# Fetching the modulation slabs four by four between weight slabs in the head of a two-block transformer kernel

## The chip, the cores and the metric

The kernel runs on one core of a Trainium2 chip. The metric is device time in microseconds (us) of one execution. The engines are TensorE (PE in the rows; PEld is its weight load), VectorE (DVE), ScalarE (ACT), GpSimd (POOL) and SyncE (SP). The rows mark with a q what an engine's queue only issues: SPq and ACTq are transfers that SyncE and ScalarE start.

## What is computed

Two layers of a first block and two of a second, over 256 tokens of width 1024, in fp32. The part that the change touches is the very start of the first layer of the first block:

```
silu_c, silu_cc = silu(c), silu(c_ctx)
shift, scale, gate = split(silu_c @ w_mod[l] + b_mod[l], 3)       # for x
shift_c, scale_c, gate_c = split(silu_cc @ w_mod[l] + b_mod[l], 3)  # for ctx
hc = rms_norm(ctx) * g_pre[l] * (1 + scale_c) + shift_c
zc = hc @ w_in[l]           # 1024 x (11*512 + 3072), then heads, attention, merge
...
ctx = ctx + gate_c * rms_norm(c_out, g_post[l])
```

`w_mod[l]` is 1024 x 3072: a third of it gives the shift, a third the scale, a third the gate. Shift and scale are needed before any column of `hc @ w_in` can be finished; the gate only when the layer closes.

## The kernel before, in words

All large matrices are fetched from HBM in slabs of 512 KB, 256 rows (two k-tiles of 128) by 512 columns. A weight slab lands in one of four places of `raw` (`SLOTS`). ScalarE copies it to `whi` (rounded to fp32r, `split`, L550), GpSimd writes the remainder `wlo = raw - whi` (L525) and raises `lo_ready`. TensorE multiplies each 128x128 tile of the activations (`hhi`, `hlo`) with `whi` and `wlo` in three products (L1890 to L1892), 12 matmuls of 512 columns to a slab, and raises `weights_used`. SyncE may fetch weight slab n only when GpSimd has finished slab n-4 (`slab`, L413), and it is one queue in order: a transfer that has to wait holds back all that are written behind it.

The first pass starts with weight slabs 0 to 11 (`first_chunks`), three chunks of columns (RK, RQ, DKc) times four slabs. Each chunk is split in two halves of k: slabs 0 to 5 are k-tiles 0 to 3 of the three chunks, (c, s) = (0,0) (0,1) (1,0) (1,1) (2,0) (2,1), and slabs 6 to 11 are k-tiles 4 to 7, (0,2) (0,3) (1,2) (1,3) (2,2) (2,3). From slab 12 on the chunks are whole: 12 to 15 are DQ, 16 to 19 RV, and so on.

The modulation slabs (`w_mod`) are counted here as M0, M1, ... M0 to M7 give shift and scale of the first half of k, M8 to M15 those of the second half; they land in eight places of `modz`, and TensorE multiplies them with the conditioning vectors (`mod_slab`, L2066). The sum is copied by ScalarE (`mod_copy`, L723), turned by TensorE (`mod_turn`, L2075), and VectorE makes `modT` of it (L1252, L1253). ScalarE and VectorE then write the high and the low part of the activations of a quarter of k (`stream_high` L613, `stream_low` L1185 and L1188), after TensorE has turned that quarter (`turn_tokens`, L1956). M16 and on are the gate columns and later chunks: they land in three places of `modw`, and VectorE accumulates them (L1219, L1221), one slab being four operations. M19 and later ones wait on SyncE until VectorE has used the slab three before (`modw_used`). `MOD_FIRST` says how many modulation slabs SyncE fetches behind each of weight slabs 0 to 11, `MOD_BESIDE` the same for later ones: in this pass M19 stands behind weight slab 12, M20 behind 13, M21 behind 15, M22 behind 17.

VectorE does stream_low of all four quarters and then M16 to M19. TensorE turns the gate rows behind weight slab 12 and waits there until M19 is used (`turn_rows`, L2122, L2125).

ScalarE's program around this: split 4, split 5, split 6, mod_copy, split 7, three transfers (const, dist, wsT), the streams of quarters 2 and 3 with splits 8 and 9 behind them, then split 10, evacuation of RK (two tiles, L754), split 11, split 12, evacuation of RQ, split 13, split 14, evacuation of DKc, split 15. Behind that come the eight exponentials of the decay tables and the reach values (`decays`, L774 and L775, `reach`, L789), with no split between them, and then splits 16, 17 and 18.

Of the kernel before, what the change touches and what calls it, by code (L numbers as in the profile page):

```python
# [143 lines left out]
def build(nc, g, out):  # L144
# [14 lines left out]
    with ExitStack() as ctx:  # L159
        def sem(name):  # L160
            return ctx.enter_context(nc.semaphore(name))
# [171 lines left out]
        mod_turned, modT_ready = sem("mod_turned"), sem("modT_ready")  # L333
# [55 lines left out]
                  (4, 0): (8, 9), (4, 1): (10, 11, 12), (4, 2): (6, 7)}  # L389
        MOD_ORDER = (0, 2, 1, 3)  # L390
        HALVES = [[(c, s) for c in range(3) for s in part] for part in ((0, 1), (2, 3))]
        MOD_FIRST = {(1, 1): 3, (2, 0): 1, (2, 1): 4, (0, 3): 1, (1, 3): 1, (2, 3): 1}
        MOD_BESIDE = {0: (12, 13, 15, 17, 22, 23, 25, 26, 30, 31, 32, 33, 35), 1: (3, 4, 5, 14, 17, 18, 22, 23),
                      3: (3, 4, 5, 18, 19, 22, 23, 24)}
        LATE = [MV, RG, DG, MU, MG]
# [12 lines left out]
        def _(sp):  # L408
            w = Tally(sp)

            def slab(mat, row, col, slot, n=CH):

                sp.wait_ge(lo_ready, w(lo_ready))  # L413
                src = mat[bass.ds(row, SLAB_K * P), bass.ds(col, n)].rearrange("(k p) n -> p k n", p=P)
                sp.dma_start(raw[:, slot, :, 0:n], src).then_inc(raw_full[slot], 16)
# [11 lines left out]
            def mod_slab():  # L427

                i = mods["n"]
                mods["n"] += 1  # L430
                l, r = divmod(i, 6 * SLOTS)
                c, q = divmod(r, SLOTS)
                if i < 4 * SLOTS:
                    c = MOD_ORDER[c]
                src = flat["w_mod"][l * D + q * SLAB_K * P:l * D + (q + 1) * SLAB_K * P, c * CH:(c + 1) * CH]
                src = src.rearrange("(k p) n -> p k n", p=P)
                if i < 4 * SLOTS:
                    if i >= MODZ:
                        sp.wait_ge(mod_used, w(mod_used))
                    sp.dma_start(modz[:, i % MODZ], src).then_inc(modz_full[i % MODZ], 16)  # L440
                else:
                    if i >= 4 * SLOTS + MODW:
                        sp.wait_ge(modw_used, w(modw_used))
                    sp.dma_start(modw[:, i % MODW], src).then_inc(modw_full[i % MODW], 16)
# [5 lines left out]
            def first_chunks():  # L450

                for n, (c, s) in enumerate(HALVES[0] + HALVES[1]):
                    slab(flat["w_in"], s * SLAB_K * P, (RK, RQ, DKc)[c], n % SLOTS)
                    for _ in range(MOD_FIRST.get((c, s), 0)):
                        mod_slab()
# [84 lines left out]
        def _(act):  # L540
            w = Tally(act)
# [6 lines left out]
            def split(slot, n=CH):  # L548
                act.wait_ge(raw_full[slot], w(raw_full[slot], 16))
                act.activation(whi[:, slot, :, 0:n], raw[:, slot, :, 0:n], ACT.Copy).then_inc(hi_ready, 1)  # L550
# [53 lines left out]
            def turned_high(scale, shift, banks=HB, quarters=range(4), high=h_pairs[0]):  # L604

                for q in quarters:
                    act.wait_ge(h_turned, w(h_turned))
                    for k in range(2 * q, 2 * q + 2):
                        part = banks[q][:, (k % 2) * S:(k % 2 + 1) * S]
                        if shift is None:  # L610
                            ins = act.activation(high[q][:, k % 2], part, ACT.Copy, scale=scale(k))
                        else:
                            ins = act.activation(high[q][:, k % 2], part, ACT.Identity, scale=scale(k), bias=shift(k))  # L613
                    ins.then_inc(h_high, 1)

            def stream_high(n, quarters):

                a = 0 if PASSES[n][0] else 1
                turned_high(lambda k: modT[:, 1, k, a:a + 1], lambda k: modT[:, 0, k, a:a + 1], HB_FIRST if n == 0 else HB_EDGE,
                            quarters, (h_ctx_pairs if n == 2 else h_pairs)[0])  # L620
# [99 lines left out]
            def mod_copy():  # L720

                act.wait_ge(mod_used, w(mod_used, 2 * SLOTS))
                act.activation(modrow[:], A[2][:, 0:MODN], ACT.Copy).then_inc(mod_copied, 1)  # L723

            def first_chunks():

                mod_copy()
                split(0)
                act.wait_ge(modT_ready, w(modT_ready))
                for q in range(2):  # L730
                    stream_high(0, (q,))
                    split(1 + q)
                split(3)
                for slot in range(2):
                    act.wait_ge(weights_used, w(weights_used))
                    split(slot)
                for slot in range(2, 4):
                    act.wait_ge(weights_used, w(weights_used))
                    split(slot)
                    if slot == 2:  # L740
                        mod_copy()
                act.dma_start(const[:, N_FIRST:], g["p_const"][:, N_FIRST:]).then_inc(consts_in, 16)
                tables(0)
                act.wait_ge(modT_ready, w(modT_ready))
                for q in range(2):
                    stream_high(0, (2 + q,))
                    act.wait_ge(weights_used, w(weights_used))
                    split(q)
                for c, col in enumerate((RK, RQ, DKc)):
                    act.wait_ge(weights_used, w(weights_used))  # L750
                    split((2 * c + 2) % SLOTS)
                    for t in range(TT):
                        act.wait_ge(projected, w(projected))
                        act.activation(z[:, t, col:col + W], (G[0:2], G[2:4], A[0:2])[c][t][:], ACT.Copy).then_inc(evacuated, 1)  # L754
                    split((2 * c + 3) % SLOTS)
# [1129 lines left out]
        def _(pe):  # L1885
            w = Tally(pe)
# [63 lines left out]
            def turn_tokens(src, banks, quarters):  # L1950

                for q in quarters:
                    for b in range(2):
                        k = 2 * q + b
                        for t in range(TT):
                            ins = pe.transpose(banks[q][:, b * S + t * P:b * S + (t + 1) * P], src[:, t, k * P:(k + 1) * P], ident)  # L1956
                    ins.then_inc(h_turned, 1)
# [120 lines left out]
            def first_chunks():  # L2078

                def part(n, c, s, fresh=False):  # L2080
                    pe.wait_ge(lo_ready, w(lo_ready))
                    if fresh:
                        pe.wait_ge(h_split, w(h_split))
                    banks = (G[0:2], G[2:4], A[0:2])[c]
                    for t in range(TT):
                        for kk in range(SLAB_K):
                            k = s * SLAB_K + kk
                            cols = slice(t * P, (t + 1) * P)
                            ins = product(banks[t][:], hhi[:, k, cols], hlo[:, k, cols], n % SLOTS, kk, CH, k == 0, k == KT - 1)
                        if s == SLOTS - 1:  # L2090
                            ins.then_inc(projected, 1)
                    if s < SLOTS - 1:
                        ins.then_inc(weights_used, 1)

                pe.wait_ge(silu_c, w(silu_c))
                for i in range(2 * SLOTS):
                    if i == 5:
                        pe.wait_ge(ident_in, w(ident_in, 16))
                        pe.wait_ge(norm_ready, w(norm_ready, TT))
                        turn_tokens(normed, HB_FIRST, (0, 1))  # L2100
                    mod_slab(A[2])
                pe.wait_ge(mod_copied, w(mod_copied))
                mod_turn(A[2], modrow)
                for r in range(28):
                    pe.transpose(A[3][:, r % 4 * P:(r % 4 + 1) * P], normed[:, 0, r % 8 * P:(r % 8 + 1) * P], ident)
                for n, (c, s) in enumerate(HALVES[0]):
                    part(n, c, s, c == 0)
                    for _ in range((0, 0, 5, 3, 0, 0)[n]):
                        mod_slab(A[2])
                    if n == 3:  # L2110
                        turn_tokens(normed, HB_FIRST, (2,))
                        pe.wait_ge(mod_copied, w(mod_copied))
                        mod_turn(A[2], modrow)
                    if n == 4:
                        pe.wait_ge(modT_ready, w(modT_ready, 2))
                        turn_tokens(normed, HB_FIRST, (3,))
                for n, (c, s) in enumerate(HALVES[1]):
                    part(n + len(HALVES[0]), c, s, c == 0)
# [545 lines left out]
```

## Time and profile before

| | |
|---|---|
| three timed runs | 1803.73, 1803.93 and 2532.1 us, median 1803.93 |
| the profiled execution | 1803.99 us, of which 1802.0 us is the span from the first to the last instruction |
| around the span | 1.99 us |
| mean granted TensorE clock | 0.999 of full speed |
| TensorE busy | 99% of the span |

The times are of the whole program; the change touches only what is queued in the first 60 us of it. All times of instructions below are from the start of the span of the profiled execution. "Idle before" in a row is the time that the engine stood still ahead of that instruction, and the arrow names who ended it.

### The profile page before, as it was taken

How to read it: one execution, taken by the hardware profiler on the slowest of the kernel's cores; microseconds unless marked ns; L12 is line 12 of the kernel's file. 1: busy time of each engine (PE TensorE's matmuls, PEld its weight loads, DVE VectorE, ACT ScalarE, POOL GpSimd, SP SyncE). 2: the span in 40 equal slices, each digit the busy share in tenths (PEclk: the TensorE clock that was granted, in tenths of full speed). 3: DMA queues.
4: the chain of work that ended last, by engine and by line, in shares of the span. 5: the costliest groups of instructions: out<-in, count | busy, mean ns of one | idle time of the engine just before them, and what ended most of it. 6: DMA issues, size and time to landing. Idle time of an engine off the chain costs nothing.

```text
span 1802.0 us, 25383 instructions
## 1 busy us (share of the span) xinstructions
PE 1782.7 (99%) x9224; PEld 1488.9 (83%) x9224; DVE 763.7 (42%) x1340; ACT 1047.3 (58%) x1560; POOL 1360.9 (76%) x573
## 2 busy tenths in 40 slices
PE   7999999999999999999999999999999999999998
PEld 4888888888888888888888878898888878888887
DVE  2782344843334546343337374321113665431112
ACT  4645675445677654466655666565555566746554
POOL 5867787866778877676879766778887865688886
PEclk9999999999999999999999999999999999999999
DMA  9875556754556667454647544556555654456663
GB/s 367 288 256 161 167 175 205 234 158 139 154 178 189 179 204 233 139 151 151 193 134 224 152 129 140 175 167 195 187 190 173 192 143 130 148 178 196 187 186 128
DMA packets 171409, 327.88 MB, mean 182 GB/s; under 512 B 10416, under 2 KB 15792, under 8 KB 171312
## 3 DMA queue, kind: packets, MB, share of 16 engines
q1 hardware_dynamic: 168272, 320.49, 57.6%
q10 hardware_dynamic: 3040, 6.06, 0.9%
q8 instruction: 66, 1.08, 0.2%
q14 instruction: 31, 0.25, 0.0%
HBM read 325.46 MB, written 1.05 MB: 181 GB/s over the span
## 4 chain that ended last, share of the span: by engine, by line
PE 67%; POOL 16%; issue 16%; ACT 0%; POOLq 0%; DVE 0%; DMA 0%; ACTq 0%; DVEq 0%
POOL wlo L525 16%; PE G L1890 15%; PE G L1892 15%; PE G L1891 15%; PE A L2596 2%; PE G L2596 2%; PE A L1890 2%; PE A L1892 2%; PE A L1891 2%; PE A L2597 1%; PE G L2597 1%; PE A L2342 1%; PE G L2364 1%; PE A L1944 1%; PE A L2227 1%
## 5 line engine op out<-in xcount | busy, mean ns | idle before, releaser
L525 POOL TENSOR_TENSOR wlo<-raw,whi 128x1024 fp32r<-128x1024 f32 (+1 forms) x568 | 1357.2, 2400 | 427.2 <-ACT whi L550 424.5
L550 ACT ACTIVATE whi<-raw 128x1024 fp32r<-128x1024 f32 (+1 forms) x568 | 593.1, 1048 | 571.6 <-PE G L1892 423.8
L1890 PE MATMUL G<-whi,hparts 128*128 128x512 f32 (+1 forms) x1472 | 582.3, 396 | 1.6 <-DVE hparts L1276 0.6
L1892 PE MATMUL G<-whi,hparts 128*128 128x512 f32 (+1 forms) x1472 | 568.2, 386 | 0.0
L1891 PE MATMUL G<-wlo,hparts 128*128 128x512 f32 (+1 forms) x1472 | 567.8, 386 | 0.0
L1890 PEld LDWEIGHTS G<-whi,hparts 128*128 128x128 f32 x1472 | 276.5, 188 | 60.3 <-issue 5.2
L1892 PEld LDWEIGHTS G<-whi,hparts 128*128 128x128 f32 x1472 | 276.4, 188 | 57.0
L1891 PEld LDWEIGHTS G<-wlo,hparts 128*128 128x128 f32 x1472 | 276.8, 188 | 50.9
L1890 PE MATMUL G<-whi,osplit 128*128 128x512 f32 x240 | 94.2, 393 | 0.0
L1892 PE MATMUL G<-whi,osplit 128*128 128x512 f32 x240 | 93.4, 389 | 0.0
L1891 PE MATMUL G<-wlo,osplit 128*128 128x512 f32 x240 | 93.4, 389 | 0.0
L1825 DVE TENSOR_TENSOR G<-G,frelu 128x512 f32<-128x512 f32 x12 | 8.4, 699 | 188.9 <-ACT frelu L1119 188.9
L1606 DVE TENSOR_REDUCE nmx<-A 128x1 f32<-128x512 f32 (+1 forms) x48 | 25.6, 595 | 112.3 <-PE A L2342 112.2
L2596 PE MATMUL A<-hparts,whi 128*128 128x512 f32 x192 | 70.0, 398 | 0.0
L2596 PE MATMUL G<-hparts,whi 128*128 128x512 f32 x192 | 69.9, 398 | 0.0
L1221 DVE SCALAR_TENSOR_TENSOR A<-modw,cond,A 128x512 f32<-128x512 f32 x84 | 60.0, 753 | 9.3 <-DMA modw<-in_w_mod 7.6
L586 ACT ACTIVATE z<-G 128x512 f32<-128x512 f32 x66 | 39.5, 599 | 33.3 <-PE G L1892 33.1
L2597 PE MATMUL A<-hparts,wlo 128*128 128x256 f32 x192 | 53.9, 281 | 0.0
L2597 PE MATMUL G<-hparts,wlo 128*128 128x256 f32 x192 | 53.9, 281 | 0.0
L1892 PEld LDWEIGHTS G<-whi,osplit 128*128 128x128 f32 x240 | 45.1, 188 | 9.4
L1890 PEld LDWEIGHTS G<-whi,osplit 128*128 128x128 f32 x240 | 45.1, 188 | 9.4 <-issue 0.3
L1891 PEld LDWEIGHTS G<-wlo,osplit 128*128 128x128 f32 x240 | 45.1, 188 | 9.1
(413 smaller groups left out, 2558.6 us busy)
## 6 DMA issues: line engine op xcount, KB each, us to landing
raw<-in_w_in SPq DMA_DIRECT2D x324, 512.0 KB, 3.8
raw<-in_w_up SPq DMA_DIRECT2D x64, 512.0 KB, 3.7
raw<-in_w_down SPq DMA_DIRECT2D x64, 512.0 KB, 3.5
raw<-in_w_out SPq DMA_DIRECT2D x40, 512.0 KB, 3.9
raw<-in_w_branch_out SPq DMA_DIRECT2D x36, 512.0 KB, 4.3
modw<-in_w_mod SPq DMA_DIRECT2D x32, 512.0 KB, 5.1
raw<-in_w_branch SPq DMA_DIRECT2D x24, 512.0 KB, 3.5
modz<-in_w_mod SPq DMA_DIRECT2D x16, 512.0 KB, 10.0
```

The costliest lines, as they stand in the source:

```text
L525: pool.tensor_tensor(wlo[:, s, :, 0:n], raw[:, s, :, 0:n], whi[:, s, :, 0:n].bitcast(F32), ALU.subtract)\
L550: act.activation(whi[:, slot, :, 0:n], raw[:, slot, :, 0:n], ACT.Copy).then_inc(hi_ready, 1)
L586: act.activation(dst[c][t], banks[t][:], func, scale=1.0 if scale is None else scale[t])\
L1221: ins = dve.scalar_tensor_tensor(kept if k == KT - 1 else bank[:], part, row, bank[:], ALU.mult, ALU.add)
L1606: ins = dve.reduce_max(nmx[:, i, b:b + 1], A[2 * i + b][:, 0:nk], AX.X, negate=True)
L1890: pe.matmul(bank, hi, whi[:, slot, kk, 0:n], start=first, stop=False)
L1891: pe.matmul(bank, hi, wlo[:, slot, kk, 0:n], start=False, stop=False)
L1892: return pe.matmul(bank, lo, whi[:, slot, kk, 0:n], start=False, stop=last)
L1944: ins = pe.transpose(A[n % 4][:, b * S + t * P:b * S + (t + 1) * P], srcs[2 * (n - bank) + b](t), ident)
L2227: ins = pe.transpose(bank[:, b * S + t * P:b * S + (t + 1) * P], z[:, t, c + h * P:c + (h + 1) * P], ident)
L2596: pe.matmul(bank, whi[:, s, kk, cols], hparts[:, :, k], start=k == 0, stop=False, skip_group_check=True)
L2597: ins = pe.matmul(bank[:, 0:S], wlo[:, s, kk, cols], hhi[:, k], start=False, stop=k == KT - 1, skip_group_check=True)
```

## The change

The modulation slabs M8 to M15 are fetched four behind weight slab 3 and four behind weight slab 4. Before it was three behind slab 3, one behind 4, four behind 5. M16, M17 and M18 are fetched behind slab 10 (one) and slab 11 (two). Before, one each stood behind slabs 7, 9 and 11. TensorE multiplies M8 to M11 behind weight slab 3 and M12 to M15 behind weight slab 4 (before: five behind slab 2, three behind slab 3). mod_turn moves from behind slab 3 to behind slab 4, and the turning of quarter 3 from behind slab 4 to behind slab 5. On ScalarE the second mod_copy moves ahead of split 6, the stream of quarter 2 ahead of split 7, and quarter 3 ahead of split 8. The number of instructions and of bytes stays.

```
-        MOD_FIRST = {(1, 1): 3, (2, 0): 1, (2, 1): 4, (0, 3): 1, (1, 3): 1, (2, 3): 1}
+        MOD_FIRST = {(1, 1): 4, (2, 0): 4, (2, 2): 1, (2, 3): 2}
...
                 for slot in range(2):
                     act.wait_ge(weights_used, w(weights_used))
                     split(slot)
+                mod_copy()
                 for slot in range(2, 4):
                     act.wait_ge(weights_used, w(weights_used))
                     split(slot)
                     if slot == 2:
-                        mod_copy()
+                        act.wait_ge(modT_ready, w(modT_ready))
+                        stream_high(0, (2,))
                 act.dma_start(const[:, N_FIRST:], g["p_const"][:, N_FIRST:]).then_inc(consts_in, 16)
                 tables(0)
-                act.wait_ge(modT_ready, w(modT_ready))
-                for q in range(2):
-                    stream_high(0, (2 + q,))
+                stream_high(0, (3,))
+                for slot in range(2):
                     act.wait_ge(weights_used, w(weights_used))
-                    split(q)
+                    split(slot)
...
                 for n, (c, s) in enumerate(HALVES[0]):
                     part(n, c, s, c == 0)
-                    for _ in range((0, 0, 5, 3, 0, 0)[n]):
+                    for _ in range((0, 0, 0, 4, 4, 0)[n]):
                         mod_slab(A[2])
                     if n == 3:
                         turn_tokens(normed, HB_FIRST, (2,))
+                    if n == 4:
                         pe.wait_ge(mod_copied, w(mod_copied))
                         mod_turn(A[2], modrow)
-                    if n == 4:
+                    if n == 5:
                         pe.wait_ge(modT_ready, w(modT_ready, 2))
                         turn_tokens(normed, HB_FIRST, (3,))
```

## Rows read from the trace of the kernel before

**Rows 1.** Page, part 1 (busy time) and part 5 (last column: idle before).

```profile
PE 1782.7 (99%) x9224; PEld 1488.9 (83%) x9224; DVE 763.7 (42%) x1340; ACT 1047.3 (58%) x1560; POOL 1360.9 (76%) x573
...
L1890 PE MATMUL G<-whi,hparts 128*128 128x512 f32 (+1 forms) x1472 | 582.3, 396 | 1.6 <-DVE hparts L1276 0.6
```

**Rows 2.** Timeline of TensorE, 30 to 76 us: start, duration, instruction, idle before.

```profile
30.97 1.93 PE L2066 MATMUL A<-modz,cond 128*32 128x256 f32 x32
33.63 0.64 PE L2066 MATMUL A<-modz,cond 128*32 128x256 f32 x8 [0.73 <-DMA modz<-in_w_mod]
...
40.47 0.62 PE L2075 MATMUL A<-const,modrow 128*128 128x16 f32 x4 [1.23 <-ACT modrow L723]
...
46.99 0.39 PE L1890 MATMUL G<-whi,hparts 128*128 128x512 f32 x1
...
66.04 1.03 PE L2125 MATMUL A<-const,modacc 128*128 128x128 f32 x8
...
75.82 0.47 PE L1890 MATMUL G<-whi,hparts 128*128 128x512 f32 x1 [0.57 <-POOL wlo L525]
```

**Rows 3.** Timeline of ScalarE, 29 to 75 us.

```profile
29.60 1.06 ACT L550 ACTIVATE whi<-raw 128x1024 fp32r<-128x1024 f32 x1 [5.20 <-DMA raw<-in_w_in]
...
39.09 1.06 ACT L550 ACTIVATE whi<-raw 128x1024 fp32r<-128x1024 f32 x1 [5.72 <-DMA raw<-in_w_in]
...
60.79 1.06 ACT L550 ACTIVATE whi<-raw 128x1024 fp32r<-128x1024 f32 x1 [1.17 <-PE A L1892]
...
63.51 0.60 ACT L754 ACTIVATE z<-A 128x512 f32<-128x512 f32 x1 [0.76 <-PE A L1892]
...
64.96 0.68 ACT L774 ACTIVATE A<-dist,lg 128x512 f32<-128x512 f32 x1
...
71.95 2.94 ACT L550 ACTIVATE whi<-raw 128x1024 fp32r<-128x1024 f32 x3
```

**Rows 4.** Stretches of 10 us: busy time by engine, clock, DMA share, GB/s.

```profile
30.00:40.00 10.00, 8.51 (x85) 4.89 (x83) 0.00 (x0) 2.63 (x3) 4.75 (x2) 1.00 1.05 387
40.00:50.00 10.00, 9.53 (x46) 7.95 (x47) 7.08 (x12) 5.42 (x9) 8.81 (x4) 1.00 1.05 397
```

**Rows 5.** Timeline of GpSimd, at 31 us.

```profile
30.74 2.37 POOL L525 TENSOR_TENSOR wlo<-raw,whi 128x1024 fp32r<-128x1024 f32 x1 [1.67 <-ACT whi L550]
```

**Rows 6.** Tile raw on SyncE's queue, around 54 and 62 us: issue and landing.

```profile
L415 SPq DMA_DIRECT2D raw<-in_w_in x1: 444/444/444, 54.0 to 54.0; - x1
...
DMA to landing us min/median/max: 6.0/6.0/6.0
...
L415 SPq DMA_DIRECT2D raw<-in_w_in x1: 367/367/367, 62.1 to 62.1; - x1
...
DMA to landing us min/median/max: 3.8/3.8/3.8
```

**Rows 7.** Transfers issued in the first 100 us: KB each, median us to landing.

```profile
dist<-in_k_dist ACTq DMA_DIRECT2D x1, 768.0 KB, 8.0
const<-in_p_const ACTq DMA_DIRECT2D x1, 456.0 KB, 6.4
...
wsT<-in_mlp_w_s ACTq DMA_DIRECT2D x1, 256.0 KB, 11.3
```

**Rows 8.** Timeline of SyncE's queue: the issue of M19 and of M20.

```profile
50.64 0.37 SPq L444 DMA_DIRECT2D modw<-in_w_mod  x1
...
53.54 0.37 SPq L444 DMA_DIRECT2D modw<-in_w_mod  x1
```

**Rows 9.** Timeline of VectorE: second half of modT, first decay operation.

```profile
41.33 1.30 DVE L1253 SCALAR_TENSOR_TENSOR modT<-modT,small 128x8 f32<-128x8 f32 x1
...
66.41 0.70 DVE L1448 TENSOR_TENSOR A<-A,e 128x512 f32<-128x512 f32 x1 [6.96 <-ACT e L775]
```

**Rows 10.** Two stretches at the end of the span, columns as in rows 4.

```profile
1796.00:1798.70 2.70, 0.00 (x0) 0.00 (x0) 1.40 (x3) 1.53 (x4) 0.00 (x0) 1.00 0.00 0
1798.70:1802.00 3.30, 0.00 (x0) 0.00 (x0) 0.24 (x1) 0.21 (x1) 0.00 (x0) 0.51 0.42 159
```

More of the change, by code:

```diff
@@ L391, in build @@
         HALVES = [[(c, s) for c in range(3) for s in part] for part in ((0, 1), (2, 3))]
-        MOD_FIRST = {(1, 1): 3, (2, 0): 1, (2, 1): 4, (0, 3): 1, (1, 3): 1, (2, 3): 1}
+        MOD_FIRST = {(1, 1): 4, (2, 0): 4, (2, 2): 1, (2, 3): 2}
         MOD_BESIDE = {0: (12, 13, 15, 17, 22, 23, 25, 26, 30, 31, 32, 33, 35), 1: (3, 4, 5, 14, 17, 18, 22, 23),
@@ L736, in first_chunks @@
                     split(slot)
+                mod_copy()
                 for slot in range(2, 4):
@@ L740, in first_chunks @@
                     if slot == 2:
-                        mod_copy()
+                        act.wait_ge(modT_ready, w(modT_ready))
+                        stream_high(0, (2,))
                 act.dma_start(const[:, N_FIRST:], g["p_const"][:, N_FIRST:]).then_inc(consts_in, 16)
                 tables(0)
-                act.wait_ge(modT_ready, w(modT_ready))
-                for q in range(2):
-                    stream_high(0, (2 + q,))
+                stream_high(0, (3,))
+                for slot in range(2):
                     act.wait_ge(weights_used, w(weights_used))
-                    split(q)
+                    split(slot)
                 for c, col in enumerate((RK, RQ, DKc)):
@@ L2107, in first_chunks @@
                     part(n, c, s, c == 0)
-                    for _ in range((0, 0, 5, 3, 0, 0)[n]):
+                    for _ in range((0, 0, 0, 4, 4, 0)[n]):
                         mod_slab(A[2])
@@ L2111, in first_chunks @@
                         turn_tokens(normed, HB_FIRST, (2,))
+                    if n == 4:
                         pe.wait_ge(mod_copied, w(mod_copied))
                         mod_turn(A[2], modrow)
-                    if n == 4:
+                    if n == 5:
                         pe.wait_ge(modT_ready, w(modT_ready, 2))
```

## The prediction

> **What bounds the kernel now.** I read the page's busy shares first, then the timelines of TensorE and of ScalarE over the first 80 us, then the DMA share in stretches of 10 us and the landing of single transfers. TensorE is busy for 1782.7 of 1802.0 us [rows 1]. So nothing in the head can win more than the idle time that TensorE has there, while a new wait costs its whole length. From the first weight slab to slab 16 TensorE stands still three times [rows 2]: 0.73 us for M12, 1.23 us for ScalarE's copy of the modulation row, and 0.57 us at 75.82 for GpSimd's slab 16. The third is of another kind. ScalarE has the decay exponentials and the reach values between split 15 and split 16: they start at 64.96 and split 16 comes at 71.95 [rows 3], 7.0 us later, and TensorE starts slab 16 at 75.82, 3.87 us after that. So the start of slab 16 hangs on the end of split 15, not on TensorE's own pace: **slab 16 starts 10.86 us after the decays start.** TensorE's commonest matmul has 1.6 us of idle time before it in the whole run, the largest part that one releaser ended being 0.6 us [rows 1]; there is nothing behind slab 16 in which a delay could vanish, so a shift of slab 16 goes to the end of the kernel whole.
>
> The second thing to see is DMA: its share is 1.05 and it moves 387 to 397 GB/s between 30 and 50 us [rows 4]. A slab of 512 KB takes 1.36 us at 387 GB/s. Landings in this stretch are thus a sum of bytes in order of issue, and any time in which the queue runs empty is lost to all that land behind.
>
> **TensorE's side.** Slabs 0 to 2 end at 30.97 as before; then came five modulation slabs with the wait of 0.73 and three more. Four modulation slabs cost 1.93 us [rows 2], a weight slab 2.72 us ((66.04 - 46.99) / 7, slabs 6 to 12 [rows 2]). With the change slab 3 runs from 30.97 to 33.7, M8 to M11 (landed by 29.6, see below) to 35.7, the turn of quarter 2 (0.7) to 36.4, slab 4 to 39.1, M12 to M15 to 41.1. ScalarE then is free and copies at once, so the wait is some 0.5 us (a copy of 0.4 and the handing over) in place of 1.23. Slab 5 runs from 42.1 to 44.9, the turn of quarter 3 to 45.5. Slab 6 then has to wait for the low part of quarter 2, whose chain is: mod_turn 42.1, modT 42.6, stream_high behind split 6 to 43.8, stream_low (two operations and a subtraction, 1.8 us) to 45.7. That takes 0.3 us back. Slab 6 starts at 45.8, before 46.99 [rows 2]. **TensorE is 1.2 us earlier** from there, and slab 12 would end at 64.8, slab 15 at 73.8. The moved instructions cost nothing more: their number is the same, they stand on the same engines.
>
> **DMA's side.** Slab 4 landed at 29.6 and slab 6 at 39.1 (ScalarE's splits start there, released by DMA [rows 3]); slab 5, with M11 between, two slabs behind slab 4 at 32.3. Now one more modulation slab is ahead of slab 4 and four more are ahead of slab 5: they land at 31.0 and 37.7; slab 6 stays at 39.1, slab 7 at 40.4, slab 8, without M16 ahead, at 41.7. But slab 9 may only be issued when GpSimd is done with slab 5. Split (1.06 [rows 3]) and remainder (2.37 [rows 5]) take 3.5 us: 41.2. The fastest landing in this stretch is 3.8 us after the issue [rows 6], so slab 9 lands at 45.0, and between 41.7 and some 43 to 45 the queue holds nothing else: slab 10 waits for slab 6 (split after mod_copy, 41.5 to 42.6, remainder to 45.1), and M16 now stands behind slab 10. ScalarE's three transfers, 456, 768 and 256 KB [rows 7], were issued from 40.46 and are now issued behind split 7, from 43.7, data from 46.0.
>
> Before, by 44.4 slab 9 and M16 had landed. Now at 46.0 slab 9 is there and M16 is not: **DMA is 1.6 us and one slab (1.4 us) behind, 3.0 us in all.** Slab 14 landed at 60.0 (issued 54.0, 6.0 us [rows 6]), with the stretch before it full. All that stands ahead of it is the same set as before, so it comes at 60.0 + 3.0 = 63.0 at the earliest. A second gate acts on top: M19 is ahead of slab 13 and M20 ahead of slab 14 in SyncE's queue, and they wait for VectorE. The issues of M19 and M20 are 2.9 us apart [rows 8], which is VectorE's pace per slab. M16 lands at about 52.6: const takes from 46.0 to 47.2, slab 10 shares the engines with dist to 50.1, M16 with what is left of dist and with wsT to 52.6. So it is used at 55.5, M17 at 58.4, M18 at 61.2. M20 is issued at 58.4, lands no earlier than 62.2, and slab 14 a slab later at 63.5. **I take 63.4 for slab 14 and 64.8 for slab 15**; the ends are 61.5 (the gap in the queue half as long, M16 1 us earlier) and 66.
>
> **What follows on ScalarE.** Before, split 14 at 60.79 waited for TensorE, not for its data [rows 3]. Now it waits for data: 63.5 to 64.5, then the two evacuations of DKc (0.6 each [rows 3]) to 65.5, split 15 (data there at 64.8) 65.5 to 66.5. The decays start at 66.45 in place of 64.96: **+1.5 us**. Slab 16 starts at 66.45 + 10.86 = 77.3 in place of 75.82. TensorE will be done with slab 15 at 73.8, so the idle time there grows from 0.57 to 3.5 us, and what was won before (1.2 us) is inside it: the net is +1.5 us. The gate rows are late as well, and here I count nothing: M19 lands at 59.4, VectorE uses it by 64.0, TensorE asks behind slab 12 at 64.8. If that cover is gone the wait falls inside the same 3.5 us. VectorE itself stood idle for 6.96 us until 66.41 in the run before [rows 9], so being busy to 64.0 doesn't delay the decays. Slabs 12 and 13 have 0.3 to 1 us to spare, by the same landings; if they are late, that too is inside the 3.5 us.
>
> Sum: 1803.99 + 1.5 = **1805.5 us**. The profiled execution stands 0.06 us above the median of the runs shown, so it is used as it is.
>
> **A rule against the row.** The second modT operation, on 8 elements to a partition, took 1.30 us [rows 9]. It ended at 42.63, with GpSimd in the middle of its work. The Trainium skill, "SBUF — State Buffer", on the shared port pair, says that VectorE and GpSimd hold a common port pair for a whole instruction and that the other blocks. The trace agrees with that. By that rule the new order is lucky: GpSimd is idle between slab 5 (41.2) and slab 6 (from 42.6) when modT is written at 42.5, and the operation should take about 0.2. If the block hits after all, the stream, split 7 and ScalarE's transfers come 1 us later, and the sum would be about +2.3 instead of +1.5.
>
> **The rivals.**
> (1) *The landings don't hold ScalarE.* If slab 14 is there by 59.6 and slab 15 by 63, split 14 follows TensorE again and everything is 1.2 us earlier: 1802.8 us. What speaks for it: slab 14 landed 0.8 us before its split in the run before, and my DMA chain is long. Against: the queue needs 3 us less than I count. The point from which it decides is slab 14's landing at 61.9: earlier wins, later loses. Chance 0.23.
> (2) *Nothing to be seen*: the two shifts cancel, decays start within 0.4 us of 64.96, 1803.6 to 1804.4. Chance 0.15.
> (3) *The clock falls in the wait.* At the end of the span TensorE has no instruction after 1796, the granted clock is 1.00 until 1798.7 and then 0.51, 1.2 GHz in place of 2.4 [rows 10]. My wait ahead of slab 16 is 3.5 us, longer than those 2.7. If the clock falls, slab 16 takes up to 5.4 in place of 2.7 us and slab 17 part of it: +1.5 to +3 us on top of the +1.5, 1807 to 1808.5. Against: no wait of this size stands between matmuls in the trace, and where it lies in time may matter. Chance 0.12. The Trainium skill, "TensorE: Matmul & The Clock Gate", says the same of idle stretches: TensorE falls to half its clock after one. It speaks against this change; rows 10 show it only at the end of work.
>
> **How the numbers follow.** The forecast, 1804.5 to 1807, has 0.50, the rivals 0.23, 0.15 and 0.12. Eight tenths lie between 1802.5 (rival 1 reached) and 1808.0 (rival 3 in most of its reach, or the block in the port). Likeliest case alone: 1804.5 to 1807. About 2% is what a measurement of this kernel can tell from no change; that would be 36 us, and no mechanism here reaches it: within 2% has 0.98, the rest is left for something unseen, slightly more to the slow side.
>
> **What would show it.** Right: the timeline of TensorE has no wait at 33 us, about 0.5 us before mod_turn at 41.5, slab 6 at 45.8; DMA share has a dip between 42 and 46 us; ScalarE's split 14 is released by DMA and not by TensorE; the decays start near 66.5; TensorE's wait for wlo ahead of slab 16 is 3 to 4 us, and no later stretch differs. Wrong: a split 14 still released by TensorE (rival 1), a granted clock below 1.00 after 74 us (rival 3), a new wait of TensorE for slab 9 or for the gate rows, or a shift that appears only after 80 us. A slab 14 later than 66 would break the range upward.

## The result, and the profile after

The changed kernel takes 1808.19 us (median of 12 runs, 1807.59 to 1809.8) against 1803.77 us, a ratio of 1.0026 with a 95% interval of 1.0018 to 1.0033: 4.4 us slower, clear of noise. The prediction took 2% for what a measurement of this kernel can tell; the interval is under 0.1% to either side. Of the kernel before, eleven of twelve runs lie between 1803.59 and 1804.20 us and one took 2532.1 us, which the median leaves out. The forecast had the sign and the place, but 1.5 us for the size; the range ended at 1808.0, just short of the measured median. The profiled execution took 1809.39 us with a span of 1807.4 us, 5.4 us more than before, so it lies at the upper end of the runs. I account for that execution first, and for the median with the experiments.

TensorE's waits in the changed kernel, 22 us to the end (engine, line, released by: us in total, times, longest):

```profile
PE G L1891 <- POOL wlo L525: 4.3, 1, 4.3
PE G L1891 <- DVE hparts L1189: 0.6, 2, 0.4
PE G L1891 <- DVE hparts L1277: 0.6, 1, 0.6
PE A L2076 <- ACT modrow L723: 0.5, 1, 0.5
```

The waits for M12 (0.73) and the long one for the modulation row (1.23) of [rows 2] are gone and a short one for the row is left (0.5), as worked out. What was 0.57 us ahead of weight slab 16 is now 4.3 us. The same place in TensorE's timeline, with the idle time before and then the length of the matmuls behind it:

```profile
73.68 0.39 PE L1893 MATMUL G<-whi,hparts 128*128 128x512 f32 x1
78.39 0.77 PE L1891 MATMUL G<-whi,hparts 128*128 128x512 f32 x1 [4.32 <-POOL wlo L525]
78.96 0.63 PE L1892 MATMUL G<-wlo,hparts 128*128 128x512 f32 x1
```

Slab 16 starts at 78.39 in place of 75.82: +2.6 us. And the matmuls behind the wait last 0.63 us in place of 0.39. Their starts are 0.43 us apart, against 0.23 before. In stretches of 2 us, the column behind the busy times is the granted clock:

```profile
74.00:76.00 2.00, 0.07 (x1) 0.00 (x0) 1.97 (x5) 2.00 (x6) 0.32 (x1) 1.00 0.11 42
76.00:78.00 2.00, 0.00 (x0) 0.00 (x0) 2.00 (x2) 2.00 (x4) 2.00 (x1) 0.85 0.00 0
78.00:80.00 2.00, 1.61 (x4) 1.35 (x5) 1.97 (x4) 1.50 (x3) 2.00 (x2) 0.50 0.30 39
80.00:82.00 2.00, 2.00 (x7) 1.52 (x6) 1.93 (x4) 0.00 (x0) 2.00 (x2) 0.50 0.72 235
82.00:84.00 2.00, 2.00 (x7) 1.51 (x6) 1.96 (x4) 0.11 (x1) 2.00 (x2) 0.50 0.79 249
84.00:86.00 2.00, 2.00 (x11) 1.70 (x10) 1.96 (x3) 1.43 (x2) 1.99 (x2) 0.94 0.87 218
```

TensorE stands still from 74.07, its clock falls from 2.4 to 1.2 GHz within the stretch 76 to 78 and comes back at the start of 84 to 86. So it works at half speed from 78.4 to about 84.2: 5.8 us in which 2.9 us of work at full speed are done. 2.6 + 2.9 = 5.5 us, the 5.4 us of the span. The Trainium skill, "TensorE: Matmul & The Clock Gate", section "What's actually happening", puts an idle stretch ahead of a fall to the half clock; here the trace agrees, between matmuls and not only at the end.

Why slab 16 is late can be read on ScalarE's timeline (compare [rows 3]):

```profile
60.93 1.06 ACT L550 ACTIVATE whi<-raw 128x1024 fp32r<-128x1024 f32 x1 [0.86 <-DMA raw<-in_w_in]
64.70 1.06 ACT L550 ACTIVATE whi<-raw 128x1024 fp32r<-128x1024 f32 x1 [2.71 <-DMA raw<-in_w_in]
...
66.62 1.06 ACT L550 ACTIVATE whi<-raw 128x1024 fp32r<-128x1024 f32 x1
...
67.56 0.70 ACT L775 ACTIVATE A<-dist,lg 128x512 f32<-128x512 f32 x1
...
74.57 2.93 ACT L550 ACTIVATE whi<-raw 128x1024 fp32r<-128x1024 f32 x3
```

Split 14, at 60.79 and released by TensorE before, is at 64.70 and released by DMA. The decays start at 67.56 in place of 64.96 (+2.6), split 16 comes 7.0 us later as before, and TensorE starts slab 16 10.83 us after the decays (10.86 in the prediction).

On SyncE's queue, M19 and M20 (compare [rows 8]) and then SyncE's waits before and after, from 22 to 75 us:

```profile
55.60 0.37 SPq L444 DMA_DIRECT2D modw<-in_w_mod  x1
56.02 0.47 SPq L415 DMA_DIRECT2D raw<-in_w_in  x1
58.50 0.37 SPq L444 DMA_DIRECT2D modw<-in_w_mod  x1
```

```profile
SPq L444 <- DVE A L1221: 4.7, 2, 2.7
```

```profile
SPq L444 <- DVE A L1222: 9.1, 3, 5.6
```

M20 is issued at 58.50 in place of 53.54, and SyncE waits 9.1 us for VectorE in place of 4.7. The queue ran empty as expected, but from 40 us on, earlier than the 42 to 46 us of the prediction (compare [rows 4]; the last two columns are DMA share and GB/s):

```profile
40.00:42.00 2.00, 1.50 (x22) 0.91 (x11) 0.17 (x1) 1.26 (x2) 0.86 (x1) 1.00 0.06 16
42.00:44.00 2.00, 2.00 (x10) 1.65 (x9) 0.80 (x4) 1.83 (x4) 1.85 (x1) 1.00 0.84 257
```

How much that costs shows at slab 12, the last weight slab ahead of M19 and M20 in the queue. Its issue and its time to landing, before and after:

```profile
L415 SPq DMA_DIRECT2D raw<-in_w_in x1: 368/368/368, 47.6 to 47.6; - x1
...
DMA to landing us min/median/max: 7.2/7.2/7.2
```

```profile
L415 SPq DMA_DIRECT2D raw<-in_w_in x1: 368/368/368, 49.6 to 49.6; - x1
...
DMA to landing us min/median/max: 8.4/8.4/8.4
```

It lands at 58.0 in place of 54.8, 3.2 us late. Slab 14 lands at 64.6 in place of 60.0, 4.6 us late (its row stands in the account of the prediction below). So 3.2 us were lost before M19 was issued, and 1.4 us behind it.

### The profile page after: what moved, and what is told of

It is laid out like the page before. It is cut to its first block, busy times and chain, and to the rows that moved or that the text cites. A ratio compares the mean times of both kernels' runs of the same rounds, so it can differ in the third digit from the quotient of the medians.

```text
span 1807.4 us, 25383 instructions
## 1 busy us (share of the span) xinstructions
PE 1785.5 (99%) x9224; PEld 1490.5 (82%) x9224; DVE 766.2 (42%) x1340; ACT 1046.2 (58%) x1560; POOL 1360.4 (75%) x573
## 4 chain that ended last, share of the span: by engine, by line
PE 66%; POOL 16%; issue 16%; ACT 0%; POOLq 0%; DVE 0%; DMA 0%; ACTq 0%; DVEq 0%
POOL wlo L525 16%; PE G L1891 15%; PE G L1893 15%; PE G L1892 15%; PE A L2598 2%; PE G L2598 2%; PE A L1891 2%; PE A L1893 2%; PE A L1892 2%; PE A L2599 1%; PE G L2599 1%; PE A L2344 1%; PE G L2366 1%; PE A L1945 1%; PE A L2229 1%
## 5 line engine op out<-in xcount | busy, mean ns | idle before, releaser
L2599 PE MATMUL A<-hparts,wlo 128*128 128x256 f32 x192 | 53.9, 281 | 0.0
L2599 PE MATMUL G<-hparts,wlo 128*128 128x256 f32 x192 | 53.9, 281 | 0.0
```

Of the source, the lines that this page charges most:

```text
L2599: ins = pe.matmul(bank[:, 0:S], wlo[:, s, kk, cols], hhi[:, k], start=False, stop=k == KT - 1, skip_group_check=True)
```

## The experiments

The times are medians of 10 or 11 runs, with the lowest and the highest in brackets; the kernel before, run beside them, stood at 1803.68 to 1803.86 us. The 95% interval of a median's ratio to it reaches 0.0009 or 0.0010 to either side, 1.6 to 1.8 us. The changed kernel, also with the filled wait, and the very last version are clear of it. A difference of 1.5 us or less is shown by no interval here; it is read from the medians and the traces.

**The clock: fill the wait.** The changed kernel with work for TensorE ahead of slab 16 (c = 2 is the chunk of slabs 16 to 19).

```
                         pe.wait_ge(evacuated, w(evacuated, TT))
+                        for r in range(36 if c == 2 else 0):
+                            pe.transpose(G[0][:, r % 4 * P:(r % 4 + 1) * P], ident, ident)
```

> The changed kernel with 36 transposes of the identity into the free bank G[0] ahead of weight slab 16 (one such transpose took 0.12 us at full clock, so 4.2 us, inside TensorE's wait of 4.3 us there). They compute nothing that is used. Theory (the wait lets the clock fall, and the slow stretch is paid on top of the late slab): the granted clock stays 1.00 after 77 us, slab 16 still starts near 78.4, the idle time ahead of it is under 1 us, and the time is that of before plus 2.6 us, 1806.4 us, with less spread between runs than 1807.6 to 1809.8. Rival (the slow stretch costs nothing, as GpSimd is behind anyway and would hold TensorE at its own pace): the time stays at 1808.2 us.

Measured: 1807.67 us (1806.81 to 1808.31). Its trace, TensorE's timeline and then stretches of 2 us:

```profile
75.47 4.09 PE L2286 MATMUL G<-const 128*128 128x128 f32 x36
79.89 0.50 PE L1891 MATMUL G<-whi,hparts 128*128 128x512 f32 x1 [0.33 <-POOL wlo L525]
```

```profile
76.00:78.00 2.00, 2.00 (x21) 2.00 (x20) 1.97 (x5) 2.00 (x4) 0.75 (x1) 1.00 0.01 2
78.00:80.00 2.00, 1.67 (x16) 1.43 (x15) 2.00 (x1) 2.00 (x5) 2.00 (x2) 1.00 0.00 0
80.00:82.00 2.00, 2.00 (x9) 1.66 (x10) 1.93 (x5) 1.07 (x3) 2.00 (x1) 1.00 0.33 81
```

The clock stays full, as expected, but the time is 1.3 us above the theory's. In this execution slab 16 starts at 79.89, 4.1 us late and not 2.6. The transposes end at 79.56 and TensorE still waits 0.33 us for GpSimd, so they are not what holds it. The program ahead of them is that of the changed kernel, so the lateness itself changes from one execution to the next. This profiled execution took 1808.1 us, 4.4 us above the median of before, and 4.1 of it is slab 16. To separate the two parts I ran the changed kernel and the filled one once more, side by side.

> The changed kernel once more, nothing edited, beside its twin with the filled wait. Theory (the extra time has two parts, a slab 16 that is 2.5 to 4.5 us late from one execution to the next with the landings, and a slow stretch that some executions have and others not): 1807.6 to 1809.8 us with a median near 1808.2; executions with a mean clock of 0.999 near 1807.8, those with 0.997 near 1809.6. Rival (the first profile was typical, 2.6 us late and 2.9 us of slow clock in each): all executions near 1809 with a clock of 0.997.

> The kernel with the 36 transposes ahead of slab 16 once more, on the chip and in the call of the unedited changed kernel. Theory: the clock never falls ahead of slab 16, and the median is 0.5 to 1.0 us under that of the unedited one, near 1807.5 us. Rival (the slow stretch costs nothing on the whole): the two medians within 0.2 us.

Measured: 1808.76 us (1807.34 to 1809.8) and 1806.89 us (1806.39 to 1807.52). The changed kernel came out 0.6 us above its expected median. The filled kernel is 1.9 us faster, more than the 0.5 to 1.0 us expected, and the runs overlap only at the lowest run of the changed kernel. Across the two sets of runs the difference was smaller, 1807.67 us against 1808.19 us, so the clock is worth 0.5 us in one comparison and 1.9 us in the other; only the second was made side by side. The mean granted clock goes with the time: of the changed kernel's ten runs, those with a mean clock of 0.999 took 1807.34, 1808.26 and 1808.48 us, those with 0.998 took 1808.35 to 1808.80, those with 0.997 took 1809.25 to 1809.80. In its twelve first runs the order is looser (0.998 stands beside times from 1807.83 to 1809.60 us). The rival (0.997 in all) is out. The profiled execution of the changed kernel took 1808.72 us this time:

```profile
79.06 0.77 PE L1891 MATMUL G<-whi,hparts 128*128 128x512 f32 x1 [4.09 <-POOL wlo L525]
```

```profile
76.00:78.00 2.00, 0.00 (x0) 0.00 (x0) 2.00 (x3) 2.00 (x3) 1.64 (x1) 1.00 0.00 1
78.00:80.00 2.00, 0.94 (x2) 0.83 (x3) 1.97 (x3) 2.00 (x5) 2.00 (x2) 0.73 0.06 3
80.00:82.00 2.00, 2.00 (x6) 1.56 (x5) 1.97 (x4) 0.18 (x2) 2.00 (x2) 0.50 0.86 246
82.00:84.00 2.00, 2.00 (x11) 1.64 (x11) 1.93 (x4) 0.38 (x1) 2.00 (x2) 0.92 0.71 171
```

Here slab 16 is 3.2 us late (79.06 against 75.82) and the slow stretch only reaches into 82 to 84, some 3.3 us, of which half is lost: 3.2 + 1.6 = 4.8 us, and the span is 4.8 us over that of before. So in the same kernel the parts are 2.6 + 2.9 in one execution and 3.2 + 1.6 in another.

**Which half of the change: gate slabs at their places of before.**

```
-        MOD_FIRST = {(1, 1): 4, (2, 0): 4, (2, 2): 1, (2, 3): 2}
+        MOD_FIRST = {(1, 1): 4, (2, 0): 4, (0, 3): 1, (1, 3): 1, (2, 3): 1}
```

> The changed kernel with M16, M17 and M18 behind weight slabs 7, 9 and 11, as before; M8 to M15 stay four and four. Theory (the loss comes from the gate slabs put late: DMA stands empty near 41 us, and VectorE starts late and holds M19, M20 and behind them slabs 13 and 14): M16 lands near 41.3, M20 is issued near 53.6, slab 14 lands near 61, the decays start near 63.9 to 64.5, no fall of the clock, 1802.8 to 1803.8 us. Rival (the four by four order alone, which brings slab 5 five us later and so slab 9 too, makes the loss): slab 14 still lands near 64, 1806 to 1808 us.

Measured: 1803.41 us (1802.97 to 1803.86), ratio 0.9998 [0.9989, 1.0007]. SyncE's wait for VectorE is 2.2 us and TensorE's wait ahead of slab 16 is 0.90 us:

```profile
SPq L444 <- DVE A L1222: 2.2, 2, 1.4
```

```profile
75.21 0.47 PE L1891 MATMUL G<-whi,hparts 128*128 128x512 f32 x1 [0.90 <-POOL wlo L525]
```

Slab 16 starts at 75.21, 0.6 us earlier than in [rows 2]. Slab 12 lands at 56.1 and slab 14 at 61.6, 1.3 and 1.6 us later than before: hardly anything is lost behind slab 12 here. The four by four order alone costs nothing that can be seen; its 0.3 us of gain are inside the interval.

**The other half alone.** The kernel before with only the gate slabs late.

```
-        MOD_FIRST = {(1, 1): 3, (2, 0): 1, (2, 1): 4, (0, 3): 1, (1, 3): 1, (2, 3): 1}
+        MOD_FIRST = {(1, 1): 3, (2, 0): 1, (2, 1): 4, (2, 2): 1, (2, 3): 2}
```

> The kernel before with only M16, M17 and M18 moved, one behind weight slab 10 and two behind 11; M8 to M15 and all programs of TensorE and ScalarE as before. Theory (late gate slabs cost only together with the empty queue that the four by four order makes): DMA share stays above 0.9 from 40 to 50 us, M16 lands near 49.5, M20 is issued near 55.3, slab 14 lands near 60.5, the decays start 64.9 to 65.4, 1803.7 to 1804.3 us. Rival (late gate slabs are the whole loss by themselves): M20 is issued near 58, slab 14 lands behind 63, 1806 to 1808 us.

Measured: 1805.09 us (1803.67 to 1807.45), between the two expectations, with the widest spread of all kernels; the ratio is 1.0008 [0.9999, 1.0017]. The theory's first claim fell: between 40 and 44 us the queue isn't full here either.

```profile
40.00:42.00 2.00, 1.85 (x10) 1.64 (x11) 1.16 (x2) 1.15 (x2) 2.00 (x1) 1.00 0.83 214
42.00:44.00 2.00, 2.00 (x13) 1.65 (x12) 0.47 (x2) 1.28 (x3) 2.00 (x2) 1.00 0.73 213
```

```profile
SPq L444 <- DVE A L1221: 10.4, 3, 6.9
```

M20 was issued at 57.4 here, two us later than I had worked out. By the medians, late gate slabs cost 1.4 us by themselves, just inside the interval; with the four by four order, which costs nothing alone, it is 4.4. The two parts don't add. I read it so: each makes the queue emptier, and the loss begins only when slabs 14 and 15 land later than ScalarE wants them.

**The gate on SyncE.** The changed kernel with M19 and M20 behind slabs 14 and 15.

```
-        MOD_BESIDE = {0: (12, 13, 15, 17, ...
+        MOD_BESIDE = {0: (14, 15, 15, 17, ...
```

> The changed kernel with M19 fetched behind weight slab 14 and M20 behind slab 15, in place of 12 and 13. Theory (SyncE's wait for VectorE ahead of M19 and M20 holds slabs 13 and 14): slab 13 lands near 59.4, slab 14 near 60.7, slab 15 near 63.4, the decays start near 64.5, TensorE waits under 1 us ahead of slab 16, the clock does not fall, 1803.4 us. Rival (the bytes that the empty queue lost hold the slabs, not the gate): slab 15 lands near 65.5, 1806 us or more.

Measured: 1804.12 us (1803.22 to 1805.12), 0.7 us above the expectation and 4.1 us under the changed kernel. M16 still lands late (M19 is issued at 56.50), and the queue is as empty at 40 to 42 us; but slabs 13 and 14 no longer stand behind SyncE's wait for VectorE, of which this is the larger part (1.0 us more is for the last operation on the gate rows):

```profile
SPq L444 <- DVE A L1222: 3.3, 3, 2.5
```

The rival's number is out, but the run does not show that the wait alone makes the loss. Slab 12 lands at 58.9, later even than in the changed kernel, so the loss of the empty stretch is still there. The edit also takes M19 and M20 out from ahead of slab 14, 1 MB or 2.7 us at 387 GB/s, and slab 14 lands at 61.6 in place of 64.6, 3.0 us earlier. What SyncE's wait costs by itself is better read from the landings: the 1.4 us between slab 12 and slab 14 above, and 0.9 to 2.0 us in the other three profiles of this order, against 3.8 to 4.4 us that slab 12 is late there already. The 0.7 us over the expectation lie in two waits that the theory did not have: TensorE now waits 0.7 us for the gate rows behind slab 12 (M19 is later), and 1.0 us for slab 16 and another.

**The stretch of decays.** One edit on ScalarE, in the changed kernel and in the kernel before. The lines left out of the cut take weight slab 16 out of the splits of its own chunk.

```
                     decays((0, 1), l)
+                    act.wait_ge(weights_used, w(weights_used))
+                    split(0)
...
                     decays((2, 3), l)
```

> The changed kernel with ScalarE's split of weight slab 16 moved ahead of the decays of heads 2 and 3 (before: behind all of them and the reach values). Theory (a late slab 15 costs what it does because slab 16 is split only behind the whole decay stretch of 7 us): TensorE's wait ahead of slab 16 falls from 4.3 to under 1.5 us, a second one of 2 to 3.5 us appears ahead of slab 17, the clock stays at 1.00, and the time is 1803.7 to 1805.3 us. Rival (slab 16 is late because its own transfer is late): the wait ahead of slab 16 stays near 4 us and the time above 1807 us.

> The kernel before with the same single edit on ScalarE, split 16 ahead of the decays of heads 2 and 3. Theory: the wait of 0.57 us ahead of slab 16 goes, slab 17 is in time, 1803.1 us, 0.6 us under before. Rival (TensorE's wait is only moved to slab 17): 1803.7 us.

Measured: 1804.32 us (1803.38 to 1806.53) and 1802.89 us (1802.69 to 1804.49). In the changed kernel the wait of 4.3 us ahead of slab 16 is gone and the longest is 1.43 us, ahead of slab 17 (the theory had 2 to 3.5 us there), and the granted clock stays at 1.00:

```profile
79.61 0.50 PE L1894 MATMUL G<-whi,hparts 128*128 128x512 f32 x1 [1.43 <-POOL wlo L525]
```

The order of the slabs in SyncE's queue is the same, and the decays start at 68.5 there, later than in the changed kernel's first profile. The edit takes 3.9 us off the changed kernel and 0.8 us off the kernel before, where the 0.57 us go. With the early split in both, the change costs 1.4 us in place of 4.4, so 3.0 us of its loss hung on the order "all decays, then split 16", the slow clock behind the long wait included.

**Something to fetch in the empty stretch.** M16 and M17 behind weight slab 8, and then the same with the early split.

```
-        MOD_FIRST = {(1, 1): 4, (2, 0): 4, (2, 2): 1, (2, 3): 2}
+        MOD_FIRST = {(1, 1): 4, (2, 0): 4, (1, 2): 2, (2, 3): 1}
```

> The changed kernel with M16 and M17 fetched behind weight slab 8, where SyncE has to wait for GpSimd's slab 5 anyway and the queue ran empty, and M18 behind slab 11. Theory (the four by four order is good by itself and what it lacked is something to fetch in the empty stretch at 41 to 43 us): M16 lands near 42.6, M17 near 44, DMA share from 40 to 44 us stays above 0.9, the decays start 63.8 to 64.5, 1802.6 to 1803.2 us. Rival (slab 5 late and so slab 9 late costs by itself): as with the gate slabs at their places of before, 1803.4 us or more.

> Both edits together: M16 and M17 behind weight slab 8, and split 16 ahead of the decays of heads 2 and 3. Theory: TensorE has no wait above 0.5 us between slab 3 and slab 24 and is 1.7 us earlier than before, 1802.0 us. Rival (GpSimd or the decay tables then hold TensorE at another slab): 1802.6 us or more.

Measured: 1803.67 us (1803.19 to 1804.53) and 1801.72 us (1801.53 to 1802.68, ratio 0.999 [0.9981, 0.9999]). Alone, the edit does what the rival said: in its profile (1803.19 us, its fastest run) the decays start at 64.1, yet over the runs it is no better than the gate slabs at their old places. Slab 15 lands at 63.1, and TensorE still waits 1.38 us for slab 16. Together with the early split no wait is left between slab 7 and slab 24; the whole list from 22 to 120 us is:

```profile
PE G L1894 <- DVE hparts L1192: 0.6, 2, 0.4
PE A L2079 <- ACT modrow L723: 0.5, 1, 0.5
```

That is the version that beats both kernels, 2.0 us under the one before. It fits the 1.2 us that the new order saves TensorE and the 0.57 us of the old wait: the 1.2 us come out only here, where the chain through ScalarE no longer takes them back.

## Why the prediction was wrong

- *Where the time is decided* (slab 16 starts 10.86 us after the decays, and nothing behind it absorbs a shift): right. 10.83 us after; the first profile's 2.6 + 2.9 us reappear in the span as 5.4. The early split bears the chain out from its other end.
- *TensorE's side* (1.2 us earlier, 0.5 us ahead of mod_turn, slab 15 done at 73.8): right. The wait for the row is 0.5 us, the two for the low parts 0.6 us together, and TensorE is through at 74.07.
- *The modT operation and the port*: right. It took 0.17 us at 42.04, GpSimd being idle until 42.15, in place of the 1.30 of [rows 9]. There it ended at 42.63, and not with GpSimd in the middle of its work, as I wrote: GpSimd had two instructions of 2.37 us from 40.22 on, and the first ended at 42.59, 0.04 us before. The Trainium skill's rule on the shared port pair ("SBUF — State Buffer", section "Who interferes with whom") held.
- *The landings*: right in kind, too small in size. **This is the first term that was mis-sized**: slab 14 at 63.4 and slab 15 at 64.8, and so +1.5 us for the decays. In the first profile they landed at 64.6 and 66.0, and the decays came 2.6 us later. DMA being 3.0 us behind was nearly right there (slab 12 is 3.2 us late). M16 came exactly at 52.6 and M20 was issued at 58.5 (58.4 worked out); then M20 needed 4.7 us and not the 3.8 us of the shortest row, and slab 14 another 1.4:

```profile
L415 SPq DMA_DIRECT2D raw<-in_w_in x1: 470/470/470, 58.9 to 58.9; - x1
...
DMA to landing us min/median/max: 5.7/5.7/5.7
```

  In the other three profiles of this order it is another step. M16 came at 53.3 to 53.9 and M20 was issued at 59.2 to 59.7; M20 then needed 3.7, 3.9 and 4.5 us, and slab 14 landed 1.8, 2.8 and 1.4 us behind it, where I had 1.3. In the filled kernel's first profile slab 14 landed at 66.2 and slab 15 at 67.5. So I had given each link of the chain about its lowest value, these never came together, and +1.5 us lay below the whole spread: the four profiles have slab 16 between 2.6 and 4.1 us late. My upper end of 66 for slab 14 was about right, but I did not carry it into the upper end of the range: 66 for slab 14 means some 4 us, 1808.0, before any clock.
- *The clock* (rival 3, chance 0.12, +1.5 to +3 us): the mechanism was right and **its weight was the second error**. It was written as a rival beside the forecast, though [rows 10] show a fall behind an idle TensorE and the forecast's own wait was 3.5 us; the sum has it at nothing. It belonged in the forecast. Measured side by side it is worth 1.9 us of the median; in the two profiles of the unfilled kernel it is 2.9 and 1.6 us. Some runs have the mean clock of the kernel before, 0.999, and lost less, but the last digit of that figure stands for 1.8 us, so it can't be said that they lost nothing. Rival 3's own reach, 1807 to 1808.5, holds the measured median, in part by luck: it had the slab 1.5 us late, and the slab was later. A clock below 1.00 after 74 us was named as a sign of being wrong, and it came.
- *Rival 1* (landings don't hold ScalarE) is what the order becomes once M19 and M20 stand behind slabs 14 and 15, or the gate slabs at their old places: 1804.12 and 1803.41 us, and not 1802.8. Slab 15 is then still near the limit: it lands at 64.3 and 63.6, just as ScalarE splits it (64.33 and 63.59).
- In hindsight, with the measured parts, +2.6 to +4.1 for the slab and up to 2.9 for the clock, the sum is 1806.6 to 1811.0, and the measured median lies in its lower half.

What stays open: why the landings of one and the same queue differ by up to 1.5 us from execution to execution (slab 15 at 66.0, 66.8, 66.6 and 67.5 in the four profiles), and how the loss divides between the bytes lost in the empty stretch and SyncE's wait over all executions. No experiment touched the first, and none separates the second.

## What to carry to other kernels

A queue that issues in order turns a slow consumer into a delay for whoever stands behind it, and any transfer ahead takes its time too: ask of every transfer that is not urgent what is written behind it, and put it behind what the busiest engine needs next. A long stretch of work without a feed in it (here 7 us of exponentials) makes the engine behind it pay for every late transfer ahead of it; one split in the middle took 0.8 us off the kernel before, where the new order alone took 0.3, and the order paid only together with it. Where every link of a chain of transfers is priced at its fastest row, the sum is a floor and not a middle. And where a change makes a wait of several us for TensorE, price the slow clock behind it as part of the forecast.

## What was not expected of the hardware

- The same idle time is followed by slow stretches of different length: with 4.3 us idle the clock fell between 76 and 78 us and was low until 84 in one execution (some 5.8 us of work at half speed), with 4.1 us idle it fell between 78 and 80 and was low until 82 to 84 in another (3.3 us).
- The spread of a kernel's time may tell of its slack. In the kernel before, ScalarE's split 14 is held by TensorE, and most runs lie within 0.6 to 0.8 us (one set reached 1.6, and one run was far off). In the changed kernel and with the gate slabs late alone it is held by DMA, and the runs spread over 2.2 to 3.8 us. With the gate slabs at their old places it waits for DMA as well, but less, and the spread is 0.9 us. This is a reading of the ranges; no run tested it.
